# Two tensors of constants placed ahead of the second pair of activation buffers, in a two-layer float32 transformer on one core

## The chip, the cores and the metric

The kernel runs on one NeuronCore of a Trainium2 chip. The metric is the device time of one execution in microseconds (us), the median of several runs. Nothing but the place of tensors in SBUF, the on-chip memory, is at issue here, so the words for it come first: SBUF has 128 partitions, a tensor takes the same range of bytes in each of them, and "the byte" of a tensor below is the first byte of that range within a partition.

## The reference

A stack of layers on two streams of 256 tokens with 1024 features: the latent tokens `x` and the context tokens `ctx`. All data are float32. One of the two layers, cut to what matters:

```python
mod = c @ w_ada + b_ada
h = modulate(rms_norm(x, g_mix), shift, scale)
u = h @ w_in
fa = fourier_mix(u_a); db = diff_attention(...); nc = neighbourhood_attention(...)
y = (g_a * (fa @ w_a) + g_b * (db @ w_b) + g_c * (nc @ w_c)) @ w_out
x = x + gate * y
...
u = dwconv3(h @ w_up, conv_w, conv_b)
a, b = split(u)
x = x + gate * ((silu(a) * b) @ w_down)
```

Behind the two layers come gated feed-forward blocks, an attention block and a sparse attention block, on the latent tokens alone. For this study the matrix products count: each is `activation @ weight`, and there are two places from which an activation comes, as told below.

## The kernel before, in words

**Split products.** TensorE takes each float32 product as three faster products (type `float32r`). An operand is held as a high part and a low part, and the sum is high·high + low·high + high·low. ScalarE makes the high part of a weight piece (L1579, `WH`), VectorE the low part (L1899, `WL`), from the raw slab that a DMA brought (`RAWB`, 1 MB each, issued by SyncE at L1098). Activations are split in the same way, into one of two pairs of buffers:

- `AH`/`AL`, the first pair, holds the normed input of a product with `w_in`, `w_up` and the like, of 8 blocks of 128 features;
- `BH`/`BL`, the second pair, holds what goes into the second product of a block: the attention outputs, the gated sum before `w_out`, and the gated hidden blocks before `w_down` (the halves 0 to 3 and 4 to 7 of its 8 blocks take turns there).

**The matmuls.** For each 128 output features TensorE runs over the k blocks of 128 inputs, with three matmuls for each (L1207, L1208, L1209, of the step kind `mm`):

```python
xh, xl = c.operand(g.src, k)
h, l = hi[:, k, s.c:s.c + 128], lo[:, k, s.c:s.c + 128]
pe.matmul(out, h, xh[:, 0:T], start=k == 0, stop=False)
pe.matmul(out, h, xl[:, 0:T], start=False, stop=False)
i = pe.matmul(out, l, xh[:, 0:T], start=False, stop=k == g.kt - 1)
```

The weight part (`h` or `l`, in `WH` or `WL`) is the stationary operand, loaded into the array with an own instruction (LDWEIGHTS, row PEld). The activation is the moving operand that streams past it, of T = 256 or 512 columns; `c.operand` gives `AH`/`AL` or `BH`/`BL`. The step kind `mm_lead` (L1224 to L1226) is the same for two outputs at once. The step kind `mm_tok` (L1242 to L1244) has the roles the other way round: the activation in `AH`/`AL` is stationary, and 256 columns of `WH`/`WL` stream past.

**Other matmuls.** Those in plain float32, such as L1304 (moving `CX`, stationary `F`) and L1315 (moving `BI`, stationary `F`), are each recorded as two instructions. The name of the moving operand comes first in the rows.

**What sets the order.** A planner (`Plan`) writes one list of steps, and every engine walks it. The planner knows of slots, banks and events, not of addresses. Waits are on semaphores that count the other engines' steps.

**Where the tensors lie.** `build` declares them one after the other, and each takes the next free bytes, rounded up to a multiple of 32. The first is `H` at byte 16512, which is 129 · 128. The sizes of `H`, `AH`, `AL`, `BH`, `BL`, `Y`, `F`, `TMP`, `SQ`, `GT`, `RS` and `BI` are all multiples of 2048 bytes, so all twelve begin at a multiple of 128. `PV` (654 numbers, 2616 bytes) takes 2624 bytes, which is 20 · 128 + 64. So what stands behind it, `CC` (1536 bytes), `CX`, `MOD` and so on to `RAWB`, `WH`, `WL` and `MB`, begins 64 bytes into a stretch of 128 (`WH` at byte 195648, `WL` at 212032); `EPS` alone begins 32 bytes further.

Of the kernel before, what the change touches and what calls it, by code (L numbers as in the profile page):

```python
# [32 lines left out]
NSM = _at  # L33
# [7 lines left out]
def _offsets(items, base=0):  # L41
    out = {}
    for n, w in items:
        out[n] = (base, base + w)
        base += w
    return out, base


OC, NCC = _offsets(_CC)
O1, NC1 = _offsets(_C1)  # L50
# [4 lines left out]
class Events:  # L55
# [5 lines left out]
    def up(self, sem, *names):  # L61
        self.count[sem] = self.count.get(sem, 0) + 1
        for name in names:
            self.when[name] = (self.sems[sem], self.count[sem])
        return self.sems[sem]
# [4 lines left out]
    def at(self, *name):  # L70
        return self.when[name] if self.whole else self.when.get(name, (None, 0))
# [890 lines left out]
class Mem:  # L962
# [23 lines left out]
    def cc(self, name):  # L986
        a, b = OC[name]
        return self.m["CC"][:, a:b]

# [71 lines left out]
    def operand(self, src, k):  # L1061
# [3 lines left out]
        if where == "A2":  # L1065
            return self.m["AH"][:, k, 256:512], self.m["AL"][:, k, 256:512]
        return self.m["BH"][:, at + k, :], self.m["BL"][:, at + k, :]

# [20 lines left out]
def sync_program(sp, on, c, plan):  # L1089

    up, at = c.ev.up, c.ev.at
    for s in plan.slabs:
        if s.j >= NR:
            old = plan.slabs[s.j - NR]
            on.wait_ge(*(at("lo", old.first + len(old.cuts) - 1) if old.cuts else at("used_raw", old.j)))
        src = c.weight(s.w)[s.k0 * 128:(s.k0 + s.kt) * 128, s.c0:s.c0 + s.cols].rearrange("(k p) c -> p k c", p=128)
        sem = c.m["rawsem"][s.j % NR]
        sp.dma_start(c.raw(s), src).then_inc(sem, 16)  # L1098
        c.ev.landed(("raw", s.j), sem, 16 * (s.j // NR + 1))
    on.wait_ge(*at("ev", ("f21", "down", 5), 7))  # L1100
    sp.dma_start(c.dram["out"], c.m["H"][:, :, 0:256]).then_inc(c.m["outsem"], 16)
    on.wait_ge(c.m["outsem"], 16)


def pool_program(pool, on, c, plan):
# [5 lines left out]
    def load(name, dst, src):  # L1111
        sem = c.m["side"][side[0]]
        side[0] += 1
        pool.dma_start(dst, src).then_inc(sem, 16)
        c.ev.landed(("side",) + name, sem, 16)

    for s in plan.steps:
        if s.kind == "load":
# [5 lines left out]
            else:  # L1124
                load((name,), {"small": c.m["PV"][:, :], "consts": c.m["CC"][:, :], "xT": H[:, :, 0:256],
                               "ctxT": H[:, :, 256:512], "consts1": CX[:, 0:NC1]}[name], dram[name])
# [19 lines left out]
        elif s.kind == "root_mul":  # L1146
            x = c.glu(s.t)
            on.wait_ge(*at("rs", s.x))
            on.wait_ge(*at("glu_silu", *s.id))
            pool.tensor_tensor(x, x, c.m["RS"][:, 0:256], ALU.mult).then_inc(up("rooted", ("root_mul",) + s.id), 1)  # L1150
        elif s.kind == "hn_turn" and s.x[0] == "nsq":
# [34 lines left out]
def tensor_program(pe, on, c, plan):  # L1186

    up, at = c.ev.up, c.ev.at
    ident, ones = c.cc("ident"), c.cc("ones")
    F, FF, BI, TMP, RS = c.m["F"], c.FF, c.m["BI"], c.m["TMP"], c.m["RS"]  # L1190
    SC = c.m["SC"]
    for s in plan.steps:
# [90 lines left out]
        elif kind == "root_turn":  # L1283
# [3 lines left out]
            for tt in range(2):  # L1287
                t = pe.transpose(c.bank(s.b)[:, tt * 128:tt * 128 + 128], RS[:, tt * 128:tt * 128 + 128], ident)
            t.then_inc(up("acc", ("root_turn", id[0])), 1)
# [273 lines left out]
def scalar_program(act, on, c, plan, nc):  # L1563

    up, at = c.ev.up, c.ev.at
    m = c.m
    F, FF, ST, EPS, H, AH, BH, Y, RS, LM = m["F"], c.FF, m["ST"], m["EPS"], m["H"], m["AH"], m["BH"], m["Y"], m["RS"], m["LM"]
    BI = m["BI"]
    for s in plan.steps:
# [51 lines left out]
        elif kind == "xroot":  # L1621
# [3 lines left out]
            for f in was:  # L1625
                on.wait_ge(*at(*f))
            to = RS[:, 256:512] if first else RS[:, 0:256]
            act.activation(to, c.bank(s.b)[:, 0:256], ACT.Sqrt, bias=EPS[:, 0:1], scale=1.0 / 1024).then_inc(
                up("acted", ("xsd", name)), 1)
            if first:  # L1630
                on.wait_ge(*at("xmean", name))
                act.activation(RS[:, 0:256], RS[:, 0:256], ACT.Sqrt, bias=EPS[:, 0:1], scale=1.0 / 1024).then_inc(
                    up("acted", ("xsd2", name)), 1)
# [85 lines left out]
        elif kind == "seq_dft":  # L1719
            l, g = id  # L1720
            on.wait_ge(*at("seq_dft", *id))
            act.activation(BH[:, g, 0:s.n], c.bank(s.b)[:, 0:s.n], ACT.Copy).then_inc(up("acted", ("fa_hi",) + id), 1)
        elif kind == "da1":
# [21 lines left out]
        elif kind == "sub_scale":  # L1745
# [8 lines left out]
            on.wait_ge(*at("sub_mul", *id))  # L1754
            act.activation(BH[:, 4 + h, 0:s.n], c.tmp(s.t)[:, 0:s.n], ACT.Copy).then_inc(up("acted", ("db_hi",) + id), 1)
        elif kind == "na1":
# [7 lines left out]
        elif kind == "na_o":  # L1764
            l, i = id
            on.wait_ge(*at("pv", "na", l, i, s.n // 128 - 1))
            on.wait_ge(*at("mark", "pe", f"da{l}"))
            act.activation(BH[:, i, 0:s.n], c.bank(s.b)[:, 0:s.n], ACT.Copy).then_inc(up("acted", ("nc_hi",) + id), 1)
        elif kind == "yh":
            l, k = id  # L1770
            on.wait_ge(*at("mark", "dve", f"merged{l}"))
            on.wait_ge(*at("mark", "pe", f"merged{l}"))
            act.activation(BH[:, k, 0:s.n], Y[:, k, 0:s.n], ACT.Copy, scale=0.5).then_inc(up("acted", ("yh_hi",) + id), 1)
        elif kind == "pair":
# [572 lines left out]
def build(nc, dram):  # L2347
    ctx = ExitStack()
    with ctx:
        def sb(name, shape, dt=F32):  # L2350
            return ctx.enter_context(nc.sbuf_tensor(name, shape, dt))

        def sem(name):
            return ctx.enter_context(nc.semaphore(name))

        mem = dict(H=sb("H", [128, 8, 512]), AH=sb("AH", [128, 8, 512], F32R), AL=sb("AL", [128, 8, 512], F32R),
                   BH=sb("BH", [128, 8, 512], F32R), BL=sb("BL", [128, 8, 512], F32R), Y=sb("Y", [128, 8, 512]),
                   F=sb("F", [128, 12, 512]), TMP=sb("TMP", [128, 4, 512]), SQ=sb("SQ", [128, 2, 512]), GT=sb("GT", [128, 2, 512]),
                   RS=sb("RS", [128, 512]), BI=sb("BI", [128, 1024]), PV=sb("PV", [128, NSM]),
                   CC=sb("CC", [128, NCC]), CX=sb("CX", [128, NC1]), MOD=sb("MOD", [128, 2, 48, 2]),  # L2360
                   G1=sb("G1", [128, 2, 8, 2]), G2=sb("G2", [128, 2, 8, 2]), ST=sb("ST", [128, 32]),
                   SC=sb("SC", [128, 56]), EPS=sb("EPS", [128, 4]), RAWB=sb("RAWB", [128, NR, SLAB]),
                   WH=sb("WH", [128, NW, PIECE], F32R), WL=sb("WL", [128, NW, PIECE], F32R),
                   MB=sb("MB", [128, 256], mybir.dt.bfloat16), NS=sb("NS", [128, 72]), LM=sb("LM", [128, 20]))
        mem["banks"] = [ctx.enter_context(nc.psum_tensor(f"PS{i}", [128, 512], F32)) for i in range(8)]
        mem["sem"] = {n: sem(n) for n in ("acc", "hi", "acted", "lo", "vec", "xlo_pool", "sums", "rooted", "pooled")}
        mem["rawsem"] = [sem(f"raw{i}") for i in range(NR)]
        mem["side"] = [sem(f"side{i}") for i in range(NSIDE)]
        mem["outsem"] = sem("stored")
        plan = Plan(Plan(None).slabs)  # L2370
        c = Mem(mem, dram, Events(mem["sem"]))
        blank = Blank()
        sync_program(blank, Once(blank), c, plan)
        pool_program(blank, Once(blank), c, plan)
        tensor_program(blank, Once(blank), c, plan)
        scalar_program(blank, Once(blank), c, plan, nc)
        vector_program(blank, Once(blank), c, plan)
        c.ev.whole, c.ev.count = True, {}
        block = ctx.enter_context(nc.Block())

        @block.sync
        def _(eng):
            sync_program(nc.sync, Once(eng), c, plan)

        @block.gpsimd
        def _(eng):
            pool_program(nc.gpsimd, Once(eng), c, plan)

        @block.tensor
        def _(eng):  # L2390
            tensor_program(nc.tensor, Once(eng), c, plan)

        @block.scalar
        def _(eng):
            scalar_program(nc.scalar, Once(eng), c, plan, nc)

        @block.vector
        def _(eng):
            vector_program(nc.vector, Once(eng), c, plan)
# [110 lines left out]
```

## Time and profile before

| | |
|---|---|
| median of 3 runs | 2776.19 us (2770.31 to 2776.48) |
| the profiled execution | 2759.57 us, its span 2757.8 us |
| TensorE (PE) busy | 2562.5 us, 93% of the span, 17840 matmuls |
| weight loads (PEld) busy | 2259.0 us, 82% |
| VectorE (DVE) busy | 1576.3 us, 57% |
| ScalarE (ACT) busy | 1219.8 us, 44% |
| GpSimd (POOL) busy | 187.4 us, 7% |
| granted TensorE clock | 0.974 of full speed, mean |
| read from HBM | 378.36 MB, 138 GB/s over the span |

All shares are of the span of one profiled execution, which was 0.6% shorter than the median of the three runs. The records of matmuls overlap, since one begins before the one ahead has drained. So the recorded duration of a matmul is longer than the time that it takes from the engine, and the distance from one start to the next is the better measure of what it costs in a dense row.

### The profile page before, as it was taken

Reading aid. Unit: us, or ns where it says so; the run is one execution under the profiler, and the core shown is the slowest. Engines: PE = TensorE matmul, PEld = TensorE weight load, DVE = VectorE, ACT = ScalarE, POOL = GpSimd, SP = SyncE. Lnnn points to the kernel's source line nnn. Section 1 sums busy time; section 2 is a strip of 40 time slices with the busy share of each in tenths; the row PEclk is TensorE's granted clock in tenths of the full one; section 3 lists DMA queues with packets and bytes.
Section 4 is the critical chain, followed back from the end, with each engine's and each line's share of the span. In section 5 each row is a group of like instructions: output and inputs, shape, how many; then the busy total and the mean of one; then the engine's idle time right before and its main releaser. Section 6 shows DMA issues by size and latency. Waiting matters only on the chain.

```text
span 2757.8 us, 42208 instructions
## 1 busy us (share of the span) xinstructions
PE 2562.5 (93%) x17840; PEld 2259.0 (82%) x17840; DVE 1576.3 (57%) x2657; ACT 1219.8 (44%) x2025; POOL 187.4 (7%) x239
## 2 busy tenths in 40 slices
PE   5997899998999998999989989999799999988999
PEld 2875577776777776878889989998799999976999
DVE  2333234545565555364668877666566675766665
ACT  3224334424333324354556554445444553555543
POOL 0000000000000000000000011010010110025100
PEclk8998999999999999999999999999899999999999
DMA  7224432231454543233354546554265456530554
GB/s 243 67 86 131 134 105 84 67 99 61 136 169 138 168 131 129 85 115 101 122 168 155 190 145 207 185 168 130 71 201 190 153 191 199 168 126 16 169 197 140
DMA packets 337387, 382.12 MB, mean 139 GB/s; under 512 B 7408, under 2 KB 301296, under 8 KB 337200
## 3 DMA queue, kind: packets, MB, share of 16 engines
q1 hardware_dynamic: 334656, 370.37, 41.2%
q0 software_dynamic: 2544, 9.06, 1.1%
q8 instruction: 141, 2.31, 0.4%
q14 instruction: 46, 0.38, 0.0%
HBM read 378.36 MB, written 1.05 MB: 138 GB/s over the span
## 4 chain that ended last, share of the span: by engine, by line
PE 77%; DVE 10%; ACT 8%; DMA 3%; issue 2%; POOL 0%; SPq 0%; DVEq 0%; ACTq 0%; POOLq 0%
PE PS L1207 20%; PE PS L1209 19%; PE PS L1208 19%; DVE WL L1899 3%; ACT WH L1579 2%; PE PS L1242 1%; PE PS L1244 1%; PE PS L1243 1%; PE PS L1255 1%; PE PS L1224 1%; DMA RAWB<-in_w_in 1%; PE PS L1225 1%; PE PS L1226 1%; PE PS L1273 1%; PE PS L1340 1%
## 5 line engine op out<-in xcount | busy, mean ns | idle before, releaser
L1899 DVE TENSOR_TENSOR WL<-RAWB,WH 128x1024 fp32r<-128x1024 f32 (+2 forms) x613 | 734.7, 1206 | 650.5 <-ACT WH L1579 649.0
L1207 PE MATMUL PS<-AH,WH 128*128 128x256 f32 (+1 forms) x2912 | 910.7, 313 | 13.8 <-DVE WL L1899 13.8
L1209 PE MATMUL PS<-AH,WL 128*128 128x256 f32 (+1 forms) x2912 | 896.6, 308 | 0.0
L1208 PE MATMUL PS<-AL,WH 128*128 128x256 f32 (+1 forms) x2912 | 896.5, 308 | 0.0
L1579 ACT ACTIVATE WH<-RAWB 128x1024 fp32r<-128x1024 f32 (+2 forms) x613 | 625.3, 1033 | 320.0 <-PE PS L1209 167.1
L1207 PEld LDWEIGHTS PS<-AH,WH 128*128 128x128 f32 x2912 | 548.9, 189 | 70.1 <-issue 22.1
L1209 PEld LDWEIGHTS PS<-AH,WL 128*128 128x128 f32 x2912 | 548.7, 188 | 31.1
L1208 PEld LDWEIGHTS PS<-AL,WH 128*128 128x128 f32 x2912 | 548.5, 188 | 29.6 <-issue 0.5
L1207 PE MATMUL PS<-BH,WH 128*128 128x256 f32 (+1 forms) x1440 | 452.2, 314 | 0.8 <-DVE WL L1899 0.8
L1209 PE MATMUL PS<-BH,WL 128*128 128x256 f32 (+1 forms) x1440 | 439.2, 305 | 0.0
L1208 PE MATMUL PS<-BL,WH 128*128 128x256 f32 (+1 forms) x1440 | 438.5, 305 | 0.0
L1207 PEld LDWEIGHTS PS<-BH,WH 128*128 128x128 f32 x1440 | 271.5, 189 | 31.8 <-issue 13.9
L1208 PEld LDWEIGHTS PS<-BL,WH 128*128 128x128 f32 x1440 | 271.2, 188 | 15.7 <-issue 3.1
L1209 PEld LDWEIGHTS PS<-BH,WL 128*128 128x128 f32 x1440 | 271.2, 188 | 14.0
L1695 ACT ACTIVATE F<-PS,PV 128x512 f32<-128x512 f32 (+1 forms) x88 | 58.4, 666 | 136.5 <-PE PS L1209 131.0
L1224 PE MATMUL PS<-AH,WH 128*128 128x256 f32 (+1 forms) x160 | 58.0, 363 | 52.1 <-DVE AL L1968 17.2
L2105 DVE SCALAR_TENSOR_TENSOR F<-PS,PV,F 128x255 f32<-128x255 f32 x132 | 63.1, 478 | 68.6 <-ACT F L1695 68.4
L2098 DVE SCALAR_TENSOR_TENSOR H<-PS,MOD,H 128x256 f32<-128x256 f32 x168 | 72.8, 478 | 48.1 <-PE PS L1209 37.4
L1242 PE MATMUL PS<-WH,AH 128*128 128x256 f32 x352 | 99.0, 281 | 0.0
L1244 PE MATMUL PS<-WH,AL 128*128 128x256 f32 x352 | 98.1, 279 | 0.0
L1243 PE MATMUL PS<-WL,AH 128*128 128x256 f32 x352 | 98.1, 279 | 0.0
L1224 PEld LDWEIGHTS PS<-AH,WH 128*128 128x128 f32 x160 | 36.4, 227 | 60.1 <-DVE AL L1968 27.6
(314 smaller groups left out, 2827.9 us busy)
## 6 DMA issues: line engine op xcount, KB each, us to landing
RAWB<-in_f_in SPq DMA_DIRECT2D x88, 1024.0 KB, 5.2
RAWB<-in_w_in SPq DMA_DIRECT2D x52, 1024.0 KB, 5.1
RAWB<-in_w_ada SPq DMA_DIRECT2D x48, 1024.0 KB, 5.4
RAWB<-in_w_up SPq DMA_DIRECT2D x44, 1024.0 KB, 5.2
RAWB<-in_f_out SPq DMA_DIRECT2D x40, 1024.0 KB, 5.1
RAWB<-in_w_down SPq DMA_DIRECT2D x20, 1024.0 KB, 5.3
RAWB<-in_sb_qkv SPq DMA_DIRECT2D x12, 1024.0 KB, 5.4
RAWB<-in_w_out SPq DMA_DIRECT2D x8, 1024.0 KB, 5.1
```

The source lines that it names most:

```text
L1207: pe.matmul(out, h, xh[:, 0:T], start=k == 0, stop=False)
L1208: pe.matmul(out, h, xl[:, 0:T], start=False, stop=False)
L1209: i = pe.matmul(out, l, xh[:, 0:T], start=False, stop=k == g.kt - 1)
L1224: pe.matmul(out[j], h, xh[:, 0:T], start=k == 0, stop=False)
L1242: pe.matmul(out, h, wh, start=k == 0, stop=False)
L1243: pe.matmul(out, h, wl, start=False, stop=False)
L1244: i = pe.matmul(out, l, wh, start=False, stop=k == 7)
L1579: act.activation(c.part("WH", p), c.raw(p.slab)[:, k0:k1, c0:c1], ACT.Copy).then_inc(up("hi", ("hi", p.p)), 1)
L1695: act.activation(c.wide(s.t, g), b[:, 0:T], ACT.Identity, bias=c.sm(f"conv_b{l}", n, 1), scale=c.sm(f"conv_w{l}", 44 + n, 1)).then_inc(up( ...
L1899: dve.tensor_tensor(c.part("WL", p), c.raw(p.slab)[:, k0:k1, c0:c1], c.part("WH", p).bitcast(F32), ALU.subtract).then_inc(up("lo", ("lo", ...
L2098: t = stt(x, b[:, q * 256:q * 256 + 256], c.mod(l, part, n, q), x, ALU.mult, ALU.add)
L2105: stt(x[:, a + 1:e], b[:, a:e - 1], c.sm(f"conv_w{l}", n, 1), x[:, a + 1:e], ALU.mult, ALU.add).then_inc(up("vec", ("upb", g.name, n, q)), 1)
```

## The change

Two declarations move: `PV` and `CC` now stand between `AL` and `BH`.

```diff
         mem = dict(H=sb("H", [128, 8, 512]), AH=sb("AH", [128, 8, 512], F32R), AL=sb("AL", [128, 8, 512], F32R),
+                   PV=sb("PV", [128, NSM]), CC=sb("CC", [128, NCC]),
                    BH=sb("BH", [128, 8, 512], F32R), BL=sb("BL", [128, 8, 512], F32R), Y=sb("Y", [128, 8, 512]),
                    F=sb("F", [128, 12, 512]), TMP=sb("TMP", [128, 4, 512]), SQ=sb("SQ", [128, 2, 512]), GT=sb("GT", [128, 2, 512]),
-                   RS=sb("RS", [128, 512]), BI=sb("BI", [128, 1024]), PV=sb("PV", [128, NSM]),
-                   CC=sb("CC", [128, NCC]), CX=sb("CX", [128, NC1]), MOD=sb("MOD", [128, 2, 48, 2]),
+                   RS=sb("RS", [128, 512]), BI=sb("BI", [128, 1024]), CX=sb("CX", [128, NC1]), MOD=sb("MOD", [128, 2, 48, 2]),
```

What each engine issues, and in which order and with which waits, is the same in both kernels, to the last instruction. The bytes of the tensors are what changes:

| tensor | byte before | byte now | into a stretch of 128: before, now |
|---|---|---|---|
| `H`, `AH`, `AL` | 16512, 32896, 49280 | the same | 0, 0 |
| `PV` | 161920 | 65664 | 0, 0 |
| `CC` | 164544 | 68288 | 64, 64 |
| `BH` | 65664 | 69824 | 0, 64 |
| `BL` | 82048 | 86208 | 0, 64 |
| `Y`, `F`, `TMP`, `SQ`, `GT`, `RS`, `BI` | 98432 to 157824 | each 4160 further on | 0, 64 |
| `CX` and all behind it, `RAWB`, `WH`, `WL` among it | 166080 on | the same | 64, 64 |

4160 is 2624 + 1536, the bytes that `PV` and `CC` take, and 32 · 128 + 64.

## Rows read from the trace of the kernel before

**Rows 1.** The profile's busy shares, and the chain that ended last.
```profile
PE 2562.5 (93%) x17840; PEld 2259.0 (82%) x17840; DVE 1576.3 (57%) x2657; ACT 1219.8 (44%) x2025; POOL 187.4 (7%) x239
PE 77%; DVE 10%; ACT 8%; DMA 3%; issue 2%; POOL 0%; SPq 0%; DVEq 0%; ACTq 0%; POOLq 0%
```

**Rows 2.** Two stretches: length, busy us (instructions) by engine, clock, DMA share, GB/s.
```profile
1658.00:1838.00 180.00, 179.06 (x1513) 178.89 (x1512) 122.83 (x189) 85.01 (x120) 17.30 (x24) 0.99 0.58 188
2000.00:2178.00 178.00, 176.72 (x1498) 176.34 (x1497) 119.27 (x179) 84.41 (x118) 17.20 (x24) 1.00 0.57 188
```

**Rows 3.** Groups by line and shape: count, busy us, mean ns, idle before.
```profile
L1207 PE MATMUL PS<-BH,WH 128*128 128x256 f32 x1120 | 316.6, 283 | 0.8 <-DVE WL L1899 0.8
...
L1207 PE MATMUL PS<-BH,WH 128*128 128x512 f32 x320 | 135.6, 424 | 0.0
...
L1224 PE MATMUL PS<-BH,WH 128*128 128x256 f32 x48 | 13.7, 284 | 2.5 <-ACT BH L1773 2.5
...
L1224 PE MATMUL PS<-BH,WH 128*128 128x512 f32 x16 | 7.6, 475 | 3.0 <-DVE BL L2069 3.0
```

**Rows 4.** Timeline of PE, 256 columns of B: start us, us, line.
```profile
1432.33 0.28 PE L1208 MATMUL PS<-BL,WH 128*128 128x256 f32 x1
...
1433.39 0.28 PE L1208 MATMUL PS<-BL,WH 128*128 128x256 f32 x1
```

**Rows 5.** The same at another time; 26 distances between these two.
```profile
1966.83 0.28 PE L1207 MATMUL PS<-BH,WH 128*128 128x256 f32 x1
...
1969.78 0.28 PE L1209 MATMUL PS<-BH,WL 128*128 128x256 f32 x1
```

**Rows 6.** Timeline of PE, `mm_tok`, two times: weights moving, activations stationary.
```profile
120.76 0.28 PE L1243 MATMUL PS<-WL,AH 128*128 128x256 f32 x1
...
121.89 0.28 PE L1244 MATMUL PS<-WH,AL 128*128 128x256 f32 x1
...
369.38 0.28 PE L1244 MATMUL PS<-WH,AL 128*128 128x256 f32 x1
...
370.44 0.28 PE L1244 MATMUL PS<-WH,AL 128*128 128x256 f32 x1
```

**Rows 7.** Plain float32 matmuls: duration ns least/median/most, first and last start.
```profile
L1315 PE MATMUL PS<-BI,F x96: 379/379/380, 92.5 to 1124.2; 128*128 128x256 f32 x96
...
L1304 PE MATMUL PS<-CX,F x48: 379/379/484, 89.0 to 1120.7; 128*128 128x256 f32 x48
```

**Rows 8.** Timeline of PE, 512 columns of B; nine distances.
```profile
624.61 0.39 PE L1207 MATMUL PS<-BH,WH 128*128 128x512 f32 x1
...
626.67 0.39 PE L1207 MATMUL PS<-BH,WH 128*128 128x512 f32 x1
```

**Rows 9.** VectorE and ScalarE on moved tensors, groups by line and shape.
```profile
L1999 DVE TENSOR_TENSOR F<-TMP 128x256 f32<-128x256 f32 x16 | 6.8, 425 | 0.5
L1996 DVE TENSOR_TENSOR TMP<-F,CX 128x256 f32<-128x256 f32 x16 | 6.7, 421 | 11.8 <-PE PS L1324 8.0 <-PE PS L1340 3.8
...
L1788 ACT ACTIVATE BH<-Y 128x256 fp32r<-128x256 f32 x56 | 23.1, 415 | 48.0 <-DVE Y L2122 48.0
...
L1682 ACT ACTIVATE F<-PS 128x256 f32<-128x256 f32 x32 | 12.2, 383 | 58.0 <-PE PS L1244 58.0
```

**Rows 10.** DMAs that land in a moved tensor or feed the weights: KB, us to landing.
```profile
RAWB<-in_f_out SPq DMA_DIRECT2D x40, 1024.0 KB, 5.1
...
BI<-in_nab POOLq DMA_DIRECT2D x16, 256.0 KB, 3.2
```

**Rows 11.** The waits, longest first: who waited for whom, us, times, longest.
```profile
DVE WL L1899 <- ACT WH L1579: 649.0, 377, 13.9
POOL BI L1114 <- DVE PS L2045: 582.5, 12, 294.5
```

## The prediction

> **What bounds the kernel now.** I read the busy shares and the chain of waits first [rows 1]. TensorE is busy for 93% of the span, the weight loads for 82%, and 77% of the chain that ended last is matmuls. VectorE (57%) and ScalarE (44%) follow. The DMA queues have 3% of the chain. So what counts is what TensorE gives to one matmul. Two long stretches show it at its densest [rows 2]: 1513 matmuls in 180 us, or 119 ns each, and 1498 in 178 us, or 119 ns each, with weight loads busy all the while and the clock at full speed (2.4 GHz, the higher of its two levels). VectorE has 57 us and more to spare in each of them, ScalarE over 90 us.
>
> Next I looked for what the change can touch. No instruction moves, no wait comes or goes. What changes is an address, and only its place in a stretch of 128 bytes can make a difference that a reader of the profile could name: the moving operands `BH` and `BL` lie 0 bytes into it now, and will lie 64 bytes into it. The weights `WH` and `WL`, against which they are multiplied, lie 64 bytes into it in both kernels. So before, the moving and the stationary operand begin in opposite halves, and after it they begin in the same half. That is so for the matmuls on B alone; those on `AH`/`AL` keep opposite halves.
>
> How many these are comes from the groups by shape [rows 3]: with 256 columns 1120 + 48 of the high·high kind, so 3 · 1168 = 3504 in all (each line of the kernel has two sisters with the same count); with 512 columns 320 + 16, so 3 · 336 = 1008.
>
> **What one of them costs.** The recorded 283 ns overlap; I take distances from start to start. At one time B's matmuls with 256 columns stand 9 distances in 1.06 us, 117.8 ns each [rows 4]. At another, the same lines with the same buffers stand 26 distances in 2.95 us, 113.5 ns each [rows 5]. Nothing differs between them that has to do with where a tensor lies, so there are two paces at one and the same address. The step kind `mm_tok` has both as well [rows 6]: 10 distances in 1.13 us, 113.0 ns, and 9 in 1.06 us, 117.8 ns. There the moving operand (weights) begins 64 bytes into the stretch, and the stationary one (activations) at 0. So a moving operand that begins 64 bytes in isn't by itself slower, and one that begins at 0 isn't by itself faster: both have the same two paces. Matmuls with 512 columns stand 9 distances in 2.06 us, 229 ns [rows 8].
>
> The Trainium skill (TensorE: Matmul & The Clock Gate, Back-to-back issue gap) gives 256 columns over 2.4 GHz plus 2.5 ns for a warm array, 109.2 ns. The trace doesn't agree, with 113 and 117.8 ns. If the new place brought B to that figure, the sum would have an estimated 3504 · 8.6 ns = 30 us less; no row shows it reached.
>
> **What the change does, part by part.**
>
> - *The moving operand begins 64 bytes in.* Rows 4, 5 and 6 price this at nothing: the same paces at 0 and at 64. I take 0 us.
> - *Moving and stationary operand begin in the same half.* No float32r row of the trace shows this, so it has bounds. The nearest rows are the plain float32 matmuls [rows 7]. L1315 streams `BI` (0 bytes in) past `F` (0), the same half. L1304 streams `CX` (64) past `F` (0), opposite halves. Both have a median of 379 ns, to the nanosecond. So there the halves cost nothing, which is why I take 0 us. But a plain float32 matmul has two recorded instructions of 379 ns, where a float32r one has one of 283 ns [rows 3, 7]; it takes its columns more slowly, so this doesn't exclude a cost. From above I take one more step of the size that the trace shows between its two paces, 117.8 − 113.5 = 4.3 ns for 256 columns, and twice that for 512: 3504 · 4.3 ns = 15.1 us, and 1008 · 8.6 ns = 8.7 us, together 23.8 us. From below I take the whole of B going at the shorter pace: 15.1 us less (an upper bound, as some go at it now), and nothing for 512 columns, since no shorter distance than 229 ns is seen as a pace there.
> - *`Y`, `F`, `TMP`, `SQ`, `GT`, `RS`, `BI` move by half a stretch too.* VectorE reads `TMP` twice in 425 ns (both 0 bytes in), and `F` with `CX` (0 and 64) in 421 ns [rows 9]. ScalarE writes B in 415 ns and `F` from PSUM in 383 ns, in pieces whose place has no trace in the numbers. Both engines have their slack from [rows 2], and VectorE's longest wait is on ScalarE's weight pieces, 649 us in 377 waits, up to 13.9 us [rows 11]. I take 0 us. If that cover were gone, 1% on VectorE's 1576 us would be 16 us.
> - *DMAs into moved tensors.* The bias tables go into `BI` in 3.2 us each, 16 of them [rows 10], and GpSimd, which issues them, waits 582 us for VectorE to be done with the old ones [rows 11]. They aren't late. The weight slabs go to `RAWB`, which doesn't move, in 5.1 us each. 0 us.
> - *`PV` and `CC`.* Their place in the stretch stays as it was. 0 us.
>
> The Trainium skill (SBUF — State Buffer, Who interferes with whom) says that TensorE has one read port for the moving operand and one for the weight load, independent of each other, and that TensorE never waits for anyone there. By that rule the sum is 0 us, and both rivals below are empty. The trace neither shows nor excludes such a wait: the two paces of [rows 4, 5] show that something holds a matmul up by 4.3 ns at unchanged addresses, and the profile doesn't name it.
>
> The sum is 0 us on the profiled execution's 2759.6 us. That execution was 16.6 us, or 0.6%, under the median of the runs, 2776.2 us, so the forecast on the median is 2776 us. A measurement of this kernel can tell about 0.3% from no change, 8.3 us. To be seen at all, the change must add or take 8.3 us / 4512 = 1.8 ns for each matmul on B.
>
> **The rivals.**
>
> *Slower: two streams from the same half.* The weight load of one matmul runs while the matmul ahead of it streams, both busy all the time [rows 2]. If the memory serves the two halves of a stretch of 128 bytes apart, opposite starts keep the two streams out of each other's way, and B's matmuls lose that. For it speaks that they take 113 to 118 ns where both streams are at work, and that all float32r pairs of the trace happen to begin in opposite halves. Against it speaks [rows 7], and that both streams cross from half to half every 16 numbers, so opposite starts don't stay opposite for long. Price: 15 to 24 us, 2791 to 2800 us. It decides from 1.8 ns for each matmul on.
>
> *Faster: B locks into the shorter pace.* The pace holds through a whole row of matmuls at once (26 distances of 113.5 ns [rows 5]), as if two rhythms fall into step at the start of the row and stay so. A moving operand that begins half a stretch later shifts one of the rhythms. That could make the shorter pace the usual one for B: 15 us less, 2761 us. A mixed row goes from A to B and back without a gap, so the step could carry over to A's matmuls; then it would be more. For it speaks that both paces exist at the same address, so the start is what decides. Against it speaks that `mm_tok`, with moving and stationary operand the other way round, also has both [rows 6]. If B were faster, the weight slabs would be next: at 188 GB/s and a DMA share of 0.58 [rows 2] they have room.
>
> *The change doesn't do what it says.* The bytes follow from the declarations, and the sizes are fixed, so B does begin 64 bytes in. What could be empty is the idea that 128 bytes is a unit of anything here. That is the forecast itself.
>
> **How the numbers follow.** No change, 2776 us: 0.53, as the rows nearest to the question [rows 6, 7] both say nothing. Slower: 0.27, since the one pairing that no row shows is the one that the change makes, and it is made for 4512 matmuls on the engine that bounds. Faster: 0.20. The likeliest case alone, with the 3 to 6 us by which the runs of one kernel differ, covers 2770 to 2782 us. The range goes from the faster case with a few us for the spread, 2757 us, to the slower case's upper end, 2800 us; a B pace that is changed by more than one step is left out, with less than 2 in 10.
>
> **What would show it.** Right: in the profile after, B's matmuls with 256 columns stand at 113 and 118 ns from start to start and with 512 at 229, as A's do; the recorded means stay at 283 and 279 ns, and TensorE's busy time at 2562 us within 5. The slower rival shows in L1207 to L1209 with `BH`/`BL` alone, their distances at 120 ns and more, and A's rows unchanged; the faster one in the same rows at 113 ns nearly throughout. If A's rows change too, or VectorE's durations on `F`, `Y` and `TMP`, then the mechanism is another than any told here. The forecast is wrong if the two medians differ by more than 8.3 us.

## The result, and the profile after

| | before | after |
|---|---|---|
| median (lowest to highest), same chip, 20 runs each | 2773.57 us (2756.89 to 2776.48) | 2778.51 us (2769.29 to 2786.57) |
| the profiled execution | 2759.57 us | 2782.18 us, its span 2780.4 us |
| granted TensorE clock in it | 0.974 | 0.967 |

The ratio of after to before is 1.0025, with a 95% interval of 1.0015 to 1.0035. So the changed kernel is slower by 0.25%, some 7 us (4 to 10). That is small, and it is not nothing. The forecast was "no change".

The busy shares of the page after, and its chain, answer to [rows 1]:

```profile
PE 2588.3 (93%) x17840; PEld 2279.6 (82%) x17840; DVE 1576.5 (57%) x2657; ACT 1219.2 (44%) x2025; POOL 187.6 (7%) x239
PE 77%; DVE 9%; ACT 8%; DMA 3%; issue 2%; POOL 0%; SPq 0%; DVEq 0%; ACTq 0%; POOLq 0%
```

VectorE, ScalarE and GpSimd are where they were, within 0.6 us, although much of what they read and write has moved. TensorE has 26 us more of recorded busy time for the same 17840 matmuls. The groups of TensorE by line and shape (count, busy us, mean ns, idle before) answer to [rows 3]:

```profile
L1207 PE MATMUL PS<-AH,WH 128*128 128x256 f32 x2176 | 617.8, 284 | 13.2 <-DVE WL L1899 13.2
...
L1207 PE MATMUL PS<-BH,WH 128*128 128x256 f32 x1120 | 319.4, 285 | 0.8 <-DVE WL L1899 0.8
...
L1207 PE MATMUL PS<-BH,WH 128*128 128x512 f32 x320 | 136.4, 426 | 0.0
```

The recorded mean of B's matmuls went from 283 to 285 ns with 256 columns, and from 424 to 426 with 512. A reader who stops here sees 2 ns and can't say whether they are real: the ends of these records are modelled, and A's matmuls with 256 columns, which the change leaves alone, went from 283 to 284. The distances from start to start tell it. They are whole rows of matmuls without a gap in between; only the first and the last record are shown, and the distances between them counted. In the timeline of TensorE after (start us, us, engine, line, what), three rows follow each other in one dense stretch, A, then B, then A:

```profile
1540.07 0.28 PE L1208 MATMUL PS<-AL,WH 128*128 128x256 f32 x1
...
1551.14 0.28 PE L1209 MATMUL PS<-AH,WL 128*128 128x256 f32 x1
...
1551.49 0.28 PE L1209 MATMUL PS<-BH,WL 128*128 128x256 f32 x1
...
1562.53 0.28 PE L1209 MATMUL PS<-BH,WL 128*128 128x256 f32 x1
...
1562.89 0.28 PE L1209 MATMUL PS<-AH,WL 128*128 128x256 f32 x1
...
1585.15 0.28 PE L1209 MATMUL PS<-AH,WL 128*128 128x256 f32 x1
```

A has 94 distances in 11.07 us, 117.8 ns each; B has 93 in 11.04 us, **118.7 ns**; A again 189 in 22.26 us, 117.8 ns. So 118.7 ns is a pace that the trace of before doesn't have: there B goes at 117.8 or at 113.5 ns [rows 4, 5]. With 512 columns the new pace is plainer. The same trace, at another time:

```profile
588.38 0.40 PE L1209 MATMUL PS<-AH,WL 128*128 128x512 f32 x1
...
598.70 0.39 PE L1209 MATMUL PS<-AH,WL 128*128 128x512 f32 x1
...
599.38 0.39 PE L1209 MATMUL PS<-BH,WL 128*128 128x512 f32 x1
...
604.26 0.40 PE L1209 MATMUL PS<-BH,WL 128*128 128x512 f32 x1
```

A: 45 distances in 10.32 us, 229 ns, as in [rows 8]. B: 21 in 4.88 us, **232.4 ns**.

Averaged over all such gapless rows of at least ten matmuls (some 3280 distances of B with 256 columns and 800 with 512, each row's first two left out), the two profiled executions give:

| mean distance, ns | A, 256 | B, 256 | `mm_tok`, 256 | A, 512 | B, 512 |
|---|---|---|---|---|---|
| before | 116.9 | 116.8 | 115.8 | 229.2 | 229.0 |
| after | 117.1 | **118.6** | 115.2 | 229.0 | **232.6** |

Only B moved clearly: 3504 · 1.8 ns = 6.3 us and 1008 · 3.6 ns = 3.6 us, together 10 us. The 1.8 ns is the upper end of what it may be. The same address gives two paces, and the share of each differs from one trace to the next, so a mean before the change of 116.8 ns stands beside others of up to 117.6 ns with the same distance between the operands (the table behind the experiments). By these the step is 1.0 to 1.8 ns, and the whole 7 to 10 us. The ratio says some 7 us, from 4 to 10.

The two profiled executions are 22.6 us apart, more than twice that. The other 12 to 13 us are not in B's pace. Before's was one of its fastest and after's one of its slower ones, and the granted clock differs (0.974 and 0.967). The repeat of the change, below, ran its profiled execution in 2774.4 us at a clock of 0.972, with B at the same 118.6 and 232.5 ns.

The other rows of before have answers that are all but unchanged: plain float32 matmuls, VectorE and ScalarE on the moved tensors (mean ns), and the waits (us, times, longest), which are 4 to 10 us longer in a span that is 23 us longer.

```profile
L1315 PE MATMUL PS<-BI,F x96: 379/379/379, 92.8 to 1130.5; 128*128 128x256 f32 x96
...
L1304 PE MATMUL PS<-CX,F x48: 379/379/483, 89.3 to 1127.0; 128*128 128x256 f32 x48
```

```profile
L1999 DVE TENSOR_TENSOR F<-TMP 128x256 f32<-128x256 f32 x16 | 6.8, 425 | 0.5
L1996 DVE TENSOR_TENSOR TMP<-F,CX 128x256 f32<-128x256 f32 x16 | 6.7, 421 | 11.8 <-PE PS L1324 8.0 <-PE PS L1340 3.8
L1788 ACT ACTIVATE BH<-Y 128x256 fp32r<-128x256 f32 x56 | 23.0, 414 | 49.8 <-DVE Y L2122 49.8
```

```profile
DVE WL L1899 <- ACT WH L1579: 658.7, 390, 13.7
POOL BI L1114 <- DVE PS L2045: 586.7, 12, 295.3
```

### The profile page after: what moved, and what is told of

Same layout as the page of the kernel before. It is cut to its first block, busy times and chain, and to the rows that moved or that the text cites. A ratio compares the mean times of both kernels' runs of the same rounds, so it can differ in the third digit from the quotient of the medians.

```text
span 2780.4 us, 42208 instructions
## 1 busy us (share of the span) xinstructions
PE 2588.3 (93%) x17840; PEld 2279.6 (82%) x17840; DVE 1576.5 (57%) x2657; ACT 1219.2 (44%) x2025; POOL 187.6 (7%) x239
## 4 chain that ended last, share of the span: by engine, by line
PE 77%; DVE 9%; ACT 8%; DMA 3%; issue 2%; POOL 0%; SPq 0%; DVEq 0%; ACTq 0%; POOLq 0%
PE PS L1207 20%; PE PS L1209 19%; PE PS L1208 19%; DVE WL L1899 3%; ACT WH L1579 2%; PE PS L1242 2%; PE PS L1243 1%; PE PS L1244 1%; PE PS L1255 1%; PE PS L1224 1%; DMA RAWB<-in_w_in 1%; PE PS L1225 1%; PE PS L1226 1%; PE PS L1273 1%; PE PS L1340 1%
## 5 line engine op out<-in xcount | busy, mean ns | idle before, releaser
L1899 DVE TENSOR_TENSOR WL<-RAWB,WH 128x1024 fp32r<-128x1024 f32 (+2 forms) x613 | 734.2, 1205 | 660.1 <-ACT WH L1579 658.7
L1207 PE MATMUL PS<-AH,WH 128*128 128x256 f32 (+1 forms) x2912 | 913.0, 314 | 14.0 <-DVE WL L1899 14.0
L1209 PE MATMUL PS<-AH,WL 128*128 128x256 f32 (+1 forms) x2912 | 899.0, 309 | 0.0
L1207 PEld LDWEIGHTS PS<-AH,WH 128*128 128x128 f32 x2912 | 550.7, 189 | 71.3 <-issue 22.2
L1209 PEld LDWEIGHTS PS<-AH,WL 128*128 128x128 f32 x2912 | 550.7, 189 | 30.9
L1207 PE MATMUL PS<-BH,WH 128*128 128x256 f32 (+1 forms) x1440 | 455.8, 317 | 0.8 <-DVE WL L1899 0.8
L1209 PE MATMUL PS<-BH,WL 128*128 128x256 f32 (+1 forms) x1440 | 443.4, 308 | 0.0
L1207 PEld LDWEIGHTS PS<-BH,WH 128*128 128x128 f32 x1440 | 272.5, 189 | 32.9 <-issue 13.9
L1209 PEld LDWEIGHTS PS<-BH,WL 128*128 128x128 f32 x1440 | 272.4, 189 | 14.6
L1224 PE MATMUL PS<-AH,WH 128*128 128x256 f32 (+1 forms) x160 | 58.0, 363 | 52.4 <-DVE AL L1968 17.2
L2128 DVE SCALAR_TENSOR_TENSOR H<-PS,H 128x256 f32<-128x256 f32 x192 | 77.4, 419 | 14.6 <-PE PS L1209 14.5
```

What stands on the lines that cost most here:

```text
L1224: pe.matmul(out[j], h, xh[:, 0:T], start=k == 0, stop=False)
L1899: dve.tensor_tensor(c.part("WL", p), c.raw(p.slab)[:, k0:k1, c0:c1], c.part("WH", p).bitcast(F32), ALU.subtract).then_inc(up("lo", ("lo", ...
L2128: stt(x, b[:, 0:256], 0.5, x, ALU.mult, ALU.add).then_inc(up("vec", ("ev", g.name, n)), 1)
```

## The experiments

All of them change only where tensors lie, but for the last one, which also changes the columns that are used. Each ran in five rounds against the kernel before on the same chip; kernels of one group shared those runs. "D" below is the byte at which the moving operand begins, minus the byte at which the stationary one begins. Two theories stood at the start: the slower rival's, that opposite or equal halves of 128 bytes decide, and its own rival, that the change's place as such costs something, for VectorE and ScalarE too. The expectations were written before each run.

### First group: is it the halves?

**e1_b_only** was meant to move B alone. `PV` goes ahead of `BH`, and small tensors are used to fill up behind `BL`.

```diff
+                   PV=sb("PV", [128, NSM]), BH=sb("BH", [128, 8, 512], F32R), BL=sb("BL", [128, 8, 512], F32R),
+                   NS=sb("NS", [128, 72]), EPS=sb("EPS", [128, 4]), Y=sb("Y", [128, 8, 512]), F=sb("F", [128, 12, 512]),
...
+                   RS=sb("RS", [128, 512]), BI=sb("BI", [128, 1024]), SC=sb("SC", [128, 56]), LM=sb("LM", [128, 20]),
```

> Only BH and BL begin 64 bytes into a stretch of 128; Y, F, TMP, SQ, GT, RS, BI are back at 0, the weights stay at 64. Theory (the same half costs the matmul): B's distances as in the changed kernel, on average 118.6 ns for 256 columns and 232.6 ns for 512, A's unchanged at 117 and 229; 1008 times 3.6 ns and 3504 times 1.6 ns, 9 us, ratio to before 1.0025 to 1.0035. Rival (the other moved tensors cost VectorE, ScalarE or plain float32 matmuls the time): B's distances at 117 and 229, ratio 1.000.

Measured: 2769.39 us against 2769.97, ratio 0.9998 (0.9983 to 1.0013). No change, and yet both buffers changed their pace. This is its timeline:

```profile
591.16 0.40 PE L1209 MATMUL PS<-AH,WL 128*128 128x512 f32 x1
...
601.66 0.40 PE L1209 MATMUL PS<-AH,WL 128*128 128x512 f32 x1
602.36 0.39 PE L1209 MATMUL PS<-BH,WL 128*128 128x512 f32 x1
...
607.13 0.39 PE L1209 MATMUL PS<-BH,WL 128*128 128x512 f32 x1
...
1554.98 0.28 PE L1208 MATMUL PS<-BL,WH 128*128 128x256 f32 x1
...
1564.82 0.28 PE L1209 MATMUL PS<-BH,WL 128*128 128x256 f32 x1
```

A with 512 columns: 45 distances in 10.50 us, 233.3 ns instead of 229. B with 512: 21 in 4.77 us, 227.1 ns, shorter than any seen before. B with 256: 82 in 9.84 us, 120.0 ns. A with 256 columns averages 114.0 ns. The reason that A changed at all: `NS` and `LM`, which stood behind the weights, now stand ahead of them, and so the weights moved by 384 bytes (3 · 128). By halves of 128 nothing happened to A. Modulo 256 it did: A's D went from 64 to 192, and B's from 64 to 0. That took the idea of a period of 128 bytes away. The parts nearly cancel: A saves 6912 · 2.9 ns = 20 us with 256 columns and loses 2304 · 4.2 ns = 10 us with 512, and B loses 3504 · 3.1 ns = 11 us.

**e2_weights_0** leaves A and B, and moves the weights by 320 bytes, with `NS` and 8 numbers of filling ahead of `WH`. D is 0 for both.

```diff
+                   RAWB=sb("RAWB", [128, NR, SLAB]), NS=sb("NS", [128, 72]), PAD32_23=sb("PAD23", [128, 8]),
```

> WH and WL begin at 0 of a stretch of 128, AH, AL, BH, BL stay at 0: all products of L1207 to L1209 have both operands in the same half, at 0. Theory (relative place counts): both A and B at 118.6 ns (256 columns) and 232.6 ns (512): (6912 + 3504) times 1.6 ns and (2304 + 1008) times 3.6 ns, 29 us, ratio 1.010. Rival (a moving operand that begins at 64 costs, wherever the weights are): A and B unchanged, ratio 1.000 or a little under.

Measured: 2789.54 us, ratio 1.0064 (1.0043 to 1.0084). Slower, as the theory of equal halves had it, but with the sizes at 512 columns on the other side: 119.9 and 120.0 ns with 256 columns for A and B, and 227.4 and 228.0 ns with 512, less than the 229 before. The time is less than expected, too: 1.0064 and not 1.010, which lies outside the interval.

**e3_weights_0_b_64** is e2 with the study's change on top: D is 0 for A and 64 for B, modulo 256.

> Weights at 0, B (and Y to BI) at 64, A at 0: B has opposite halves again, the other way round, A has the same half. Theory (relative place): B back at 117 and 229 ns, A at 118.6 and 232.6: 6912 times 1.6 ns and 2304 times 3.6 ns, 19 us, ratio 1.007. Rival (moving operand at 64 costs by itself): B at 118.6 and 232.6, A at 117 and 229, ratio 1.003.

Measured: 2786.13 us, ratio 1.0054 (1.0035 to 1.0072). A at 119.9 and 227.3 ns; B at 117.6 and 229.0 ns, before's paces. So **B's own place isn't what costs**: it lies where the changed kernel has it, and goes at the old pace, as the weights have moved too.

**e4_all_64** puts `PV` ahead of `AH`, so that A and B both have D = 128, the value that B has in the changed kernel.

```diff
+        mem = dict(H=sb("H", [128, 8, 512]), PV=sb("PV", [128, NSM]), AH=sb("AH", [128, 8, 512], F32R),
```

> PV alone moves ahead of AH: A and B begin at 64, the weights at 64. Theory (relative place): as with all at 0, A and B at 118.6 and 232.6 ns, 29 us, ratio 1.010. Rival (moving operand at 64 costs by itself): the same 1.010, so this run tells the theories apart only together with the run that has all at 0. A third theory (the distance of 4160 bytes between old and new place of B counts, not the half): here B lies 2624 bytes on and A too, so paces other than 118.6 and 232.6 would show.

Measured: 2791.30 us, ratio 1.0073 (1.0053 to 1.0092), again less than the 1.010 that was expected. Its timeline shows the changed kernel's pace in both buffers:

```profile
1529.47 0.28 PE L1209 MATMUL PS<-AH,WL 128*128 128x256 f32 x1
...
1551.89 0.29 PE L1209 MATMUL PS<-AH,WL 128*128 128x256 f32 x1
1552.26 0.28 PE L1209 MATMUL PS<-BH,WL 128*128 128x256 f32 x1
...
1563.29 0.28 PE L1209 MATMUL PS<-BH,WL 128*128 128x256 f32 x1
```

189 distances in 22.42 us and 93 in 11.03 us, 118.6 ns each; 232.5 ns with 512 columns for both.

### Second group: which step, and what of the other tensors?

**e5_control** keeps D = 64 for A and B, but shifts B by 4096 bytes and puts `Y` and what follows it 64 bytes in, as the change does (`BI` ahead of `BH`, `PV` and `CC` behind `BL`).

```diff
+                   BI=sb("BI", [128, 1024]), BH=sb("BH", [128, 8, 512], F32R), BL=sb("BL", [128, 8, 512], F32R),
+                   PV=sb("PV", [128, NSM]), CC=sb("CC", [128, NCC]), Y=sb("Y", [128, 8, 512]),
```

> BI moves ahead of BH, PV and CC ahead of Y: BH and BL lie 4096 bytes on, so at 0 of 128 again, Y to RS at 64, weights as before. Theory (the distance from the start of the weights to the start of the moving operand, modulo 256, sets the pace; it is 64 here, as before, for A and B): all distances as before, 117 ns and 229 ns, ratio 1.000 within its interval. Rival (the other moved tensors, or the absolute place of B, cost time): ratio 1.002 to 1.003.

Measured: 2767.07 us against 2772.47, ratio 0.9985 (0.9966 to 1.0004). All paces are within 0.2 ns of before's (117.0 for A and B; 229.0 for both with 512 columns). The place of `Y`, `F`, `TMP`, `SQ`, `GT` and `RS` costs nothing.

Three kernels then filled the table in steps of 32 bytes: **e6_a192_b224** (`G1` ahead of `AH`, `EPS` ahead of `BH`), **e7_a32_b96** (`SC` ahead of `AH`, `PV` ahead of `BH`) and **e8_a160_b192** (`G1` ahead of `AH`, `NS` ahead of `BH`, which moves the weights too). The label gives A's and B's D.

> Distance modulo 256: 192 for A, 224 for B (before: 64 and 64). Theory (the distance modulo 256 sets the pace; what was seen is 0: 120.0 and 227.5 ns, 64: 113 or 118 and 229, 128: 118.9 and 232.6, 192: mostly 113 and 233.3): A at 114 ns with 256 columns and 233.3 with 512, tok steps (distance 64) at 113 or 118, time of A 6912 times 3 ns less and 2304 times 4.3 ns more, 11 us less; B at 224 wasn't seen: between its neighbours, 114 to 120 and 227.5 to 233.3. If only whole 64 bytes count, B is like 192. Ratio 0.993 to 0.999. Rival (place within 128 counts, so that A is as before): A at 117 and 229.

> Distance modulo 256: 32 for A, 96 for B. Theory (distance modulo 256): A between 0 (120.0, 227.5 ns) and 64 (117, 229), B between 64 and 128 (118.9, 232.6); if only whole 64 bytes count, A as at 0 and B as at 64. Ratio 0.999 to 1.006. A pace outside of the neighbours' would say that the pace isn't a smooth matter of the distance.

> Distance modulo 256: 160 for A, 192 for B; the weights themselves begin 32 bytes further into a stretch of 64 than in any other run. Theory (distance modulo 256, absolute place without effect): B at 113 to 114 ns with 256 columns and 233.3 with 512, as A had at 192 in the run with B alone moved; A between 128 (118.9, 232.6) and 192. Rival (absolute place matters): B at 192 differs from A at 192. Ratio 0.993 to 1.003.

Measured: e6 2767.01 us, 1.0002 (0.9981 to 1.0023); e7 2794.30 us, 1.0091 (1.0061 to 1.0120); e8 2790.45 us, 1.0077 (1.0047 to 1.0107). The paces are in the table below. All three ratios lie above the ranges that were expected, e6's by little. In e7, B at D = 96 goes at 120.0 and 233.4 ns, outside of what both neighbours have (117 and 118.9; 229 and 232.6), and A at D = 32 has 233.4 ns with 512 columns, above both of its own neighbours (227.5 and 229). In e8, A at D = 160 has 118.0 and 234.3 ns, the latter above both neighbours, and B at D = 192 averages 115.4 ns, not 113 to 114. So the pace isn't a smooth matter of D: a value that wasn't measured can't be read off its neighbours. With e7 the place alone costs 22 us, about three times what the change does.

### Third group: the change alone, the change again, and the other way

**e9_b_only_true** is what e1 was meant to be: D is 64 for A and 128 for B, and `Y` to `BI` stay 0 bytes into their stretch of 128 (`G1` ahead of `AH`; `PV` ahead of `BH`; `EPS` and `NS` behind `BL`).

> B alone at distance 128 modulo 256 from the weights, as in the changed kernel; A and the weights move together, so A stays at 64; Y, F, TMP, SQ, GT, RS, BI begin at 0 of 128 as before. Theory (distance modulo 256): B at 118.9 ns (256 columns) and 232.6 ns (512), A at 117 and 229, ratio 1.002 to 1.004, the whole effect of the change. Rival (the effect hangs on the other moved tensors): B at 117 and 229, ratio 1.000.

**e10_change_again** is the changed kernel itself, beside the others.

> The changed kernel itself, on the same chip as the three others. Every theory expects what was measured for it: ratio 1.0015 to 1.0035, B at 118.6 and 232.6 ns.

Measured: e9 2775.78 us against 2770.37, ratio 1.0024 (1.0011 to 1.0036); e10 2776.97 us, ratio 1.0027 (1.0015 to 1.0039). Paces of B: 118.7 and 232.5 ns in e9, 118.6 and 232.5 in e10. With B at D = 128 and `Y` to `BI` at their old place in a stretch of 128, the whole effect is there, so nothing else of the change is needed for it.

**e11_all_192** puts `G1` (128 bytes) ahead of `AH` and does nothing else. All that stood between the two places of `G1` moves on by 128 bytes, the weights stay, and D is 192 for A and B.

```diff
+        mem = dict(H=sb("H", [128, 8, 512]), G1=sb("G1", [128, 2, 8, 2]), AH=sb("AH", [128, 8, 512], F32R),
```

> G1 (128 bytes) moves ahead of AH, so that A and B both lie at distance 192 modulo 256, the weights stay. Theory (distance modulo 256): 256 columns at 114 to 115.5 ns, 512 columns at 233.3 ns; 10416 times about 2.4 ns less and 3312 times 4.3 ns more, 25 us less and 14 us more, ratio 0.996. A theory by which the place in a stretch of 128 counts (unchanged here, all at 0) expects 1.000.

Measured: 2764.51 us, ratio 0.9982 (0.9966 to 0.9997), between 2755.1 and 2782.4 in single runs. That is faster, but by less than the 0.996 that was expected. Its timeline at the place where e4 and the changed kernel were read:

```profile
1545.06 0.28 PE L1209 MATMUL PS<-AH,WL 128*128 128x256 f32 x1
...
1558.32 0.28 PE L1209 MATMUL PS<-AH,WL 128*128 128x256 f32 x1
1558.66 0.28 PE L1209 MATMUL PS<-BH,WL 128*128 128x256 f32 x1
...
1569.20 0.28 PE L1209 MATMUL PS<-BH,WL 128*128 128x256 f32 x1
```

117 distances in 13.26 us and 93 in 10.54 us, 113.3 ns each. With 512 columns both stand at 233.3 ns, which gives back some of it: 3312 · 4.3 ns = 14 us.

**e12_192_for_256_columns** takes the better of both. The tensors stay where they are. Activations of 256 columns are written to and read from columns 32 to 287 of their block of 512, 128 bytes further on, so their D is 192; those of 512 columns keep D = 64. The three matmuls of `mm` for a product of 256 columns then read as here (`wcols` gives the columns); the high and low parts are written there to match. Some products with 256 columns, above all those out of blocks that were written 512 wide, stay at D = 64 (`A0` in the cut).

```diff
+            return self.m["AH"][:, k, wcols(at)], self.m["AL"][:, k, wcols(at)]
+        if where == "A0":
             return self.m["AH"][:, k, 0:at], self.m["AL"][:, k, 0:at]
...
-        return self.m["BH"][:, at + k, :], self.m["BL"][:, at + k, :]
+        return self.m["BH"][:, at + k, wcols(T)], self.m["BL"][:, at + k, wcols(T)]
```

> Layout as before, but where an activation has 256 columns it is written to and read from the columns 32 to 287 of its block and not 0 to 255, which puts the moving operand at distance 192; 512 columns stay at 64, and so do the first layers' matmuls that share a block of 512 and the block f11, which shares A with the keys' input. Theory: shifted matmuls at 114 to 115.5 ns, 512 columns at 229, nothing given back; some 8500 matmuls times 2 to 2.5 ns, 17 to 21 us less, ratio 0.992 to 0.994, faster than both kernels.

Measured: **2757.18 us** (2752.65 to 2764.83) against 2770.37, ratio 0.9950 (0.9932 to 0.9967). It is faster than both kernels of this study, by 13 us than the one before. Its profiled execution was one of its two slowest (2764.82 us), and shows that two paces are still there. Lines are 11 further on; L1220 is L1209 of before, and L1235 is L1224, of `mm_lead`:

```profile
1543.67 0.28 PE L1220 MATMUL PS<-BH,WL 128*128 128x256 f32 x1
...
1554.62 0.28 PE L1220 MATMUL PS<-BH,WL 128*128 128x256 f32 x1
...
1959.30 0.28 PE L1235 MATMUL PS<-BH,WH 128*128 128x256 f32 x1
...
1969.74 0.28 PE L1220 MATMUL PS<-BH,WL 128*128 128x256 f32 x1
```

93 distances of 117.7 ns, and 92 of 113.5 ns. The means are 116.7 ns (A) and 115.7 ns (B) with 256 columns, and 229.2 and 229.0 ns with 512. So 512 columns kept their pace, as expected, but the 114 to 115.5 ns of the shifted matmuls did not come: a quarter of A's distances stand in rows at 113.4 ns, where e11 has nearly three quarters, and the ratio lies just above the 0.992 to 0.994 that was expected. The kernel is faster, clear of the spread of both; that D = 192 is the cause of all of it isn't shown by this trace, whose means account for 6 us of the 13.

### What all traces say together

Mean distances by D modulo 256, over the gapless rows of each trace. In `mm_tok` the weights move and the activations stand, so its D is the weights' byte minus the activation's; it follows the same table. The weights themselves began 64, 96, 128 or 192 bytes into a stretch of 256 in these kernels, and where several kernels have the same D with the weights at different places, their paces agree as closely as the table shows. That 256 is enough as the period shows in D = 64: it is 64 modulo 512 in before, and 320 in e3's B and e9's A.

| D mod 256 | 256 columns, ns | 512 columns, ns | seen in |
|---|---|---|---|
| 0 | 119.9 to 120.0 | 227.3 to 228.0 | e1 B, e2 A and B, e3 A; `mm_tok` in e2, e3 |
| 32 | 117.3 | 233.4 | e7 A |
| 64 | 116.8 to 117.6 (rows at 113.3 and 117.8) | 229.0 to 229.2 | before A and B, after A, e3 B, e5, e9 A, e10 A; `mm_tok` in e1, e6, e11 (116.1 to 117.4) |
| 96 | 120.0 | 233.4 | e7 B; `mm_tok` in e8 |
| 128 | 118.6 to 119.0 | 232.5 to 232.6 | after B, e4 A and B, e9 B, e10 B; `mm_tok` in e4 |
| 160 | 118.0 | 234.3 | e8 A |
| 192 | 114.0 to 115.5 (rows at 113.3 and 117.8) | 233.3 to 233.4 | e1 A, e6 A, e8 B, e11 A and B; `mm_tok` in before, after, e5, e9, e10 (114.4 to 115.8) |
| 224 | 118.3 | 233.2 | e6 B; `mm_tok` in e7 |

The times of whole kernels follow the paces, though not one to one. The float32r matmuls number 6912 on A with 256 columns, 3504 on B, 1056 in `mm_tok`, and 2304 and 1008 on A and B with 512. Counts times each trace's own mean distances give between 2090 us (e11) and 2135 us (e4). The profiled executions' times follow this sum over the 14 traces with a correlation of 0.93, and what lies outside the sum is 667 us on average, with a standard deviation of 5.6 us. Nine of them:

| | sum of paces, us | profiled execution, us | the rest, us | clock |
|---|---|---|---|---|
| e11 | 2090.0 | 2768.1 | 678.2 | 0.971 |
| e12 | 2093.0 | 2764.8 | 671.8 | 0.968 |
| e1 | 2098.4 | 2769.2 | 670.8 | 0.968 |
| before | 2098.1 | 2759.6 | 661.5 | 0.974 |
| after | 2108.9 | 2782.2 | 673.3 | 0.967 |
| e10 | 2110.7 | 2774.4 | 663.8 | 0.972 |
| e2 | 2129.8 | 2790.2 | 660.3 | 0.971 |
| e7 | 2128.8 | 2799.2 | 670.4 | 0.971 |
| e4 | 2134.7 | 2793.4 | 658.7 | 0.974 |

It also parts the 22.6 us between the two profiled executions: 10.8 us are in the paces, 11.8 us in the rest, of which before has one of the smaller values and after one of the larger ones. That goes with their clocks, loosely: over the 14 traces, clock and rest have a correlation of -0.6.

Against the medians, which single out no execution, the sum claims too much. It puts e2, e3 and e4 at 32, 24 and 37 us above before, and their medians stand 20, 16 and 21 us above it. It puts the change at 11 to 13 us (after, e9, e10), and the medians say 5 to 7. All of the 13 comparisons but e11 come out lower than their sum, by 7 us on average, and they move by 0.78 us for each us of the sum. Part of the 7 us may lie in the one trace of before: its execution is 10 to 14 us under the medians, and the share of the two paces in a usual execution isn't known. So D sets the pace, or the two paces, of a dense row, and with them the rough size of a kernel's time; why the medians move less than the sums isn't shown.

## Why the prediction was wrong, point by point

- *What bounds the kernel: TensorE, and what it gives to one matmul.* Right. The kernels' times follow this distance, with a correlation of 0.93.
- *A moving operand that begins 64 bytes in costs nothing.* Right, and now shown without the other cases: e3's B lies where the changed kernel has it and goes at 117.6 and 229.0 ns.
- *"Moving and stationary operand begin in the same half. … So there the halves cost nothing, which is why I take 0 us."* **This is the step that failed.** It rested on the nearest rows, the plain float32 matmuls [rows 7], at 379 ns for either pairing. They stay at 379 ns after the change too, although L1304's own D went from 64 to 0 by it. From start to start they take 216 ns per record in dense rows, at each of the three D that they have in the traces (0, 64, and 192 for L1315 in e5), for the 256 columns that a float32r matmul takes in 113 to 120 ns. So these rows, at about half the rate, didn't show what holds up the faster ones. The prediction said so ("this doesn't exclude a cost") and then took the 0 all the same. What the runs put in its place is 1.0 to 1.8 ns for each of 3504 matmuls and 3.6 ns for each of 1008, 7 to 10 us, where the ratio has some 7.
- *The bounds, 4.3 ns and twice that.* They held, with the value at 0.4 of them at most. The point from which it decides, 1.8 ns per matmul over all 4512, lies in the middle of what was found: 7 to 10 us are 1.6 to 2.2 ns, and the measured 7 us stay just under its 8.3.
- *The slower rival, two streams from the same half.* Right in the place (`BH`/`BL` in L1207 to L1209 alone, A unchanged) and in the sign, wrong in the mechanism and in the size. Equal halves of 128 bytes have D = 0 or 128 modulo 256, and these two differ (120.0 and 118.7 ns; 227.6 and 232.5 ns). Opposite halves have D = 64 or 192, and these differ more (117.0 and 114.6 ns; 229 and 233.3 ns). It is the distance between the two operands modulo 256 that decides.
- *The faster rival, B locks into the shorter pace.* Wrong for this change. But its idea, that the offset of the two streams sets how often a row takes the shorter pace, is what D = 192 shows in e11: A's rows average 114.6 ns, where before's average 116.9.
- *The other moved tensors, the DMAs, `PV` and `CC`: 0 us.* Right. e5 moves them (`BI` by another distance) without a cost, and e9 leaves `Y` to `BI` at their place in the stretch and has the whole of it.
- *The Trainium skill's independent ports (SBUF — State Buffer, Who interferes with whom), by which the sum is 0 us.* The runs don't agree with the 0: with nothing changed but the bytes at which tensors begin, the mean distance of two matmuls goes from 114.0 ns (e1's A) to 120.0 ns (e2's B). Whether it is at a port that they wait, no run shows. The Trainium skill's figure for the gap of a matmul by itself (TensorE: Matmul & The Clock Gate, Back-to-back issue gap), 109.2 ns for 256 columns, isn't reached at any of the eight values of D.
- *The range, 2757 to 2800 us.* It held the time, 2778.5. *"The forecast is wrong if the two medians differ by more than 8.3 us":* they differ by 5, and the ratio's interval still leaves out 1. More runs told a smaller difference than I had counted on. That 2776 us came within 3 us of the result is luck in part: it stood on before's median of three runs, which is 2773.6 us over twenty.

**What stays open.** No run says what in the chip has the period of 256 bytes, nor why 256 and 512 columns rank the distances differently (D = 0 is, with 96, the slowest for 256 and the fastest for 512). Nor is it known what lets a row at D = 64 or 192 start in the shorter or the longer pace, why e12 took the shorter one so much less often than e11, or why the times move by less than the sum of the paces. Steps finer than 32 bytes weren't tried, and the high and low parts (`AH` apart from `AL`, `WH` apart from `WL`, 16384 bytes apart each, a multiple of 256) weren't moved singly.

## What to carry to other kernels

In a kernel that TensorE bounds with float32r matmuls back to back, the byte distance between the moving and the stationary tensor, modulo 256, is a setting like any other: the layouts that were tried moved this kernel from 0.998 to 1.009 of its time, with no instruction changed, and shifting the columns as well brought 0.995. Inserting a small tensor ahead of a large one shifts it unseen, so compare two layouts by it before reading a small difference as the effect of something else. And when a row of another operation is to price a doubtful cost at zero, ask first whether that operation runs at a rate at which the cost could show.

## What the hardware showed that I had not expected

- The pace of float32r matmuls has a period of 256 bytes in the distance of their operands, with 113.3 to 120.0 ns for 256 columns and 227.3 to 234.3 ns for 512.
- At D = 64 and 192 there are two paces at one and the same address, 113.3 and 117.8 ns with 256 columns, and a row keeps the one that it started with (189 distances of 117.8 ns in the changed kernel, and no change of pace within any of A's rows in the trace of before). At the other values no row at 113 ns stands in the traces, but some have two paces closer together: 118.7 and 120.0 ns in e4's A, 116.7 and 117.8 in e7's, 117.3 and 118.7 in e8's. With 512 columns D = 64 has a rare second pace too, 233.3 ns, in one row of 93 distances in the trace of before.
- The two paces don't explain how far the runs of one kernel scatter. Of the kernels with six runs, e2, e4 and e7 have no pace of 113 ns in A or B and spread by 5.6, 6.3 and 12.2 us from lowest to highest; e3 and e8, whose B has it, spread by 6.0 and 7.6 us.
- The recorded duration of a matmul hides nearly all of it (283 against 285 ns); the distances show it.
